# The PEER stage of a two-block kernel: top-k per token tile, last gate tile read by VectorE first, column gating and the split of h in pieces between the v columns

## The reference, cut to what matters

```python
def chunk(xc):                                      # 128 tokens
    q = (xc @ w_pq).reshape(P_CHUNK, P_HEADS, 2, P_DK // 2)
    s = jnp.einsum('thpd,hpkd->thpk', q, sub_keys)
    s_top, i_top = lax.top_k(s, P_TOPK)
    cand = s_top[..., 0, :, None] + s_top[..., 1, None, :]
    best, ci = lax.top_k(cand.reshape(P_CHUNK, P_HEADS, P_TOPK * P_TOPK), P_TOPK)
    e1 = jnp.take_along_axis(i_top[..., 0, :], ci // P_TOPK, axis=-1)
    e2 = jnp.take_along_axis(i_top[..., 1, :], ci % P_TOPK, axis=-1)
    expert = e1 * N_KEYS + e2
    gate = jax.nn.softmax(best.astype(jnp.float32), axis=-1).astype(xc.dtype)
    act = jax.nn.gelu(jnp.einsum('thkd,td->thk', u_tab[expert], xc), approximate=False)
    return jnp.einsum('thk,thkd->td', gate * act, v_tab[expert])
```

## Time and profile before

| | |
|---|---|
| median of three runs | 1895.78 us (1894.33 to 1897.16) |
| profiled execution, own time | 1899.66 us |
| profiled execution, span from first to last instruction | 1897.6 us |
| TensorE (PE) | busy 95% of the span |
| VectorE (DVE) | busy 54% |
| ScalarE (ACT) | busy 33% |
| GpSimd (POOL) | busy 8% |
| mean granted TensorE clock, as a share of full speed | 0.978 |
| scores | 464.95 to 472.3 us of the span |
| early u on TensorE | 473.47 to 598.05 us |
| gates and middle u on TensorE | 604.80 to 747.6 us |
| early v on TensorE | 751.95 to 928.8 us |
| main columns on TensorE | 928.8 to 1309.7 us |

### The profile page before, as it was taken

One profiled execution on the slowest core, in us unless ns is written; L12 is line 12 of the kernel. 1 busy time (PEld: TensorE's weight loads), 2 busy tenths in 40 slices (PEclk: granted clock), 3 DMA queues, 4 the chain that ended last, 5 costly groups with the idle time before them and its releaser, 6 DMA issues. The chain is left out here.

```text
span 1897.6 us, 23793 instructions
## 1 busy us (share of the span) xinstructions
PE 1806.9 (95%) x9024; PEld 1404.1 (74%) x9024; DVE 1031.9 (54%) x2060; ACT 623.3 (33%) x891; POOL 159.4 (8%) x81
## 2 busy tenths in 40 slices
PE   7999989999998999899999999998997979999997
PEld 4887556778887998677888888887776868555554
DVE  2669745220998876777776767675324532411112
ACT  2110354012012665333454545454264130122222
POOL 1100000000002996100000000000000000000000
PEclk9999999999999999999999999999998999899998
DMA  9366121333441223455555555556322244399992
GB/s 365 148 252 266 67 89 45 133 108 137 173 159 67 89 89 103 163 181 195 178 185 191 184 192 181 194 179 237 129 101 89 89 166 191 137 424 427 428 427 84
DMA packets 33335, 343.61 MB, mean 181 GB/s; under 512 B 3952, under 2 KB 4464, under 8 KB 5104
## 3 DMA queue, kind: packets, MB, share of 16 engines
q1 hardware_dynamic: 32256, 340.16, 47.5%
q10 hardware_dynamic: 1008, 2.45, 0.3%
HBM read 340.49 MB, written 2.10 MB: 181 GB/s over the span
## 5 line engine op out<-in xcount | busy, mean ns | idle before, releaser
L554 PE MATMUL psD<-xh,ring 128*128 128x256 f32 x1856 | 411.0, 382 | 8.9 <-DVE arena L2037 5.6
L554 PEld LDWEIGHTS psD<-xh,ring 128*128 128x128 f32 x1856 | 351.5, 191 | 67.0 <-issue 15.4
L839 PE MATMUL psY<-ring_r,work_r 128*128 128x512 f32 x1536 | 370.6, 397 | 11.2 <-DVE ring_r L1825 11.2
L839 PEld LDWEIGHTS psY<-ring_r,work_r 128*128 128x128 f32 x1536 | 283.1, 190 | 80.7 <-issue 18.0
L1122 ACT ACTIVATE arena<-psD 128x512 f32<-128x512 f32 (+4 forms) x187 | 132.2, 715 | 616.1 <-PE psD L554 473.2
L1122 ACT ACTIVATE ring_r<-ring 128x1024 fp32r<-128x1024 f32 x196 | 200.2, 1055 | 173.5 <-PE psY L839 113.1
L825 PE MATMUL psD<-xh_r,ring_r 128*128 128x512 f32 x544 | 194.1, 397 | 0.0
L554 PE MATMUL psD<-arena,ring 128*128 128x256 f32 x704 | 167.6, 398 | 12.2 <-DMA ring<-in_w_in 4.8
L1825 DVE TENSOR_TENSOR ring_r<-ring,ring_r 128x1024 fp32r<-128x1024 f32 x128 | 160.7, 1255 | 15.1 <-ACT ring_r L1122 15.0
L554 PEld LDWEIGHTS psD<-arena,ring 128*128 128x128 f32 x704 | 133.6, 192 | 44.7 <-issue 8.8
L827 PE MATMUL psD<-xh_r,ring_r 128*128 128x256 f32 x544 | 152.6, 280 | 0.0
(11 more groups left out here) (264 smaller groups left out, 1999.6 us busy)
## 6 DMA issues: line engine op xcount, KB each, us to landing
ring<-in_tables SPq DMA_DIRECT2D x68, 1024.0 KB, 4.8
arena<-in_experts SPq DMA_DIRECT2D x30, 2048.0 KB, 16.4
ring<-in_w_in SPq DMA_DIRECT2D x20, 2048.0 KB, 8.5
ring<-in_experts SPq DMA_DIRECT2D x18, 2048.0 KB, 14.3
ring<-in_early_v SPq DMA_DIRECT2D x30, 1024.0 KB, 4.8
ring<-in_w_mod SPq DMA_DIRECT2D x12, 2048.0 KB, 8.3
ring<-in_early_u SPq DMA_DIRECT2D x9, 2048.0 KB, 7.9
ring<-in_mid_u SPq DMA_DIRECT2D x12, 1024.0 KB, 4.9
```

The source lines that it names most:

```text
L554: last = nc.tensor.matmul(dst, a, b, start=(i == 0), stop=(i == len(pairs) - 1))
L839: last = nc.tensor.matmul(psY[:, t * D + h * 512:t * D + (h + 1) * 512], wgt[:, b, t * P:(t + 1) * P], v[:, h * 512:(h + 1) * 512], start= ...
```

## The change

The top-k of token tile 0 may begin when its four score tiles are copied, not all eight; the wait for all eight moves to the first place that overwrites their source. The exponentials of token tile 1 are taken two GELUs earlier. Both settings of `psY` to zero go; instead the first matmul into each bank of `psY` overwrites it (`start=first and i == 0`). TensorE does 17 instead of 6 middle steps before the first gate product and 5 or 6 before each of the others (`mid_done`, `LEAD`). After the last gate product VectorE reads `psD` first and ScalarE second, where it was the other way round, and the first v columns' rounding and rest stand before it. The gating of the middle columns goes from three instructions of 8 columns to two of 4 and eight of 2, one behind a v column. The split of `h` goes from two instructions to sixteen, each over an eighth of `h`, and each waits for a certain v column (`v_done`). The constants of the waits on these semaphores follow.

```diff
@@ tensor: gates and middle u @@
+def mid_done(n):
+    return LEAD + (MID * K - LEAD) * n // (T // 8) if n else 0      # LEAD = 12
...
-            pe.wait_ge(y_zero, 1)
             for n in range(T // 8):
-                for i in range(MID * K * n // (T // 8), MID * K * (n + 1) // (T // 8)):
+                for i in range(mid_done(n), mid_done(n + 1)):
                     mid_step(i)
@@ tensor: v columns @@
-                    for wgt, v in ((wgt_hi, v_hi[b]), (wgt_hi, v_lo), (wgt_lo, v_hi[b])):
+                    for i, (wgt, v) in enumerate(((wgt_hi, v_hi[b]), (wgt_hi, v_lo), (wgt_lo, v_hi[b]))):
...
-                                                    start=False, stop=False, skip_group_check=True)
+                                                    start=first and i == 0, stop=False, skip_group_check=True)
...
-            pe.wait_ge(y_zero, 2)
-            with pe.Fori(0, PRE // 4) as it:
+            pe.wait_ge(mid_ready, MID // 2)
+            for e in range(8):
+                early_v(e, e, e == 0)
+            with pe.Fori(1, PRE // 4) as it:
...
-            pe.wait_ge(h_split, 1)
+            pe.wait_ge(h_split, K)
@@ scalar @@
-            act.wait_ge(tile_free["act"], readers[:TILE["scores"] + 8].count("act"))
-            act.sem_inc(sc_ready, 1)
+                if g == 3:
+                    act.wait_ge(tile_free["act"], readers[:TILE["scores"] + n + 1].count("act"))
+                    act.sem_inc(sc_ready, 1)
...
-                if n in (TOPU // 3, TOPU // 2 - 1):
-                    t = n // (TOPU // 2 - 1)
+                if n in (TOPU // 3, TOPU // 2 - 3):
+                    t = n // (TOPU // 2 - 3)
...
-                gates_out(it, h)
+                if n + 1 < T // 8:
+                    gates_out(it, h)
                 if n + 2 < T // 8:
                     one_hot(it + 1, h)
+                else:
+                    act.wait_ge(col_loaded[0], 16 + MID_LOADS[0])
+                    act.wait_ge(gb_done, n + 3)
+                    fn(v_hi[h], early_half(col_slot, h), ACT.Copy).then_inc(v_hi_ready, 1)
+            gates_out(T // 16 - 1, 1, early_gated)
@@ gpsimd @@
-            pool.wait_ge(mid_gated, 2)
             pool.wait_ge(mid_used, MID // 2)
-            nc.gpsimd.tensor_copy(h_hi, hT).then_inc(h_hi_ready, 1)
-            pool.wait_ge(h_hi_ready, 1)
-            nc.gpsimd.tensor_tensor(h_lo, hT, h_hi.bitcast(F32), ALU.subtract).then_inc(h_split, 1)
+            pool.wait_ge(mid_gated, 6)
+            for k in range(K):
+                pool.wait_ge(v_done, 12 + 2 * k)
+                nc.gpsimd.tensor_copy(h_hi[:, k, :], hT[:, k, :]).then_inc(h_hi_ready, 1)
+                pool.wait_ge(v_done, 13 + 2 * k)
+                pool.wait_ge(h_hi_ready, k + 1)
+                nc.gpsimd.tensor_tensor(h_lo[:, k, :], hT[:, k, :], h_hi[:, k, :].bitcast(F32),
+                                        ALU.subtract).then_inc(h_split, 1)
@@ vector @@
-            dve.wait_ge(sc_ready, 1)
...
             for t in range(TT):
+                dve.wait_ge(sc_ready, t + 1)
...
-            dve.wait_ge(stat_used, STATS.index("x1") + 1)
-            nc.vector.memset(psY[:, :], 0.0).then_inc(y_zero, 1)
...
             gate_early(T // 16 - 1, 0)
-            dve.wait_ge(mid_ready, MID // 2)
-            nc.vector.memset(psY[:, 1024:2048], 0.0).then_inc(y_zero, 1)
-            gate_early(T // 16 - 1, 1)
-            dve.wait_ge(gate_copied, T // 8 + 2)
...
+            early_rest(0, 0)
+            gate_early(T // 16 - 1, 1, gb_done)
             dve.wait_ge(early_gated, T // 8 + 2)
-            for e in range(8):
-                early(e, e, False)
-                if e in (1, 3, 5):
-                    mid_gate((2, 0, 1)[e // 2])
-            dve.wait_ge(mid_gated, 3)
-            with dve.Fori(1, PRE // 4) as it:
+            for e in range(2):
+                weights_split(e, e, gate_all[:, e, :])
+                if e:
+                    early_rest(1, 1)
+            dve.wait_ge(gate_copied, T // 8 + 2)
+            dve.wait_ge(mid_ready, MID // 2)
+            mid_gate(2, 0, 4)
+            for e in range(2, 16):
+                early(e, e % 8)
+                if e == 2:
+                    mid_gate(2, 4, 4)
+                if 4 <= e < 12:
+                    mid_gate((e - 4) // 4, 2 * (e % 4), 2)
+            dve.wait_ge(mid_gated, 10)
+            with dve.Fori(2, PRE // 4) as it:
```

58 lines of the change are left out of this document (30 added, 28 removed).

## The result

The changed kernel takes 1880.44 us (median of 5 runs, 1874.07 to 1882.78), the kernel before 1896.07 us (5 runs in turn with them, 1894.33 to 1900.3). The ratio is 0.9904, with a 95% interval of 0.9888 to 0.9919. The forecast was 1877.9 us with a range of 1873.5 to 1885.5.

What follows compares the result with a forecast made beforehand. TensorE has work in 95% of the span, so only its pauses and low-clock stretches can be won. Gains of 20.75 less losses of 2.85 give net 17.9, from 1895.78 to 1877.9 us, range 1873.5 to 1885.5.

Steps and rivals of the forecast that it cites:

- The hand-over: From early u to the gates: first middle step starts near 600.8 instead of 604.80, 4.0 us gained.
- The first middle steps at the lower clock: First 12 passes of middle steps after the hand-over: 2.55 us back if the clock stays up in the shorter pause.
- Last gate product to column 0: Between the last gate product and v column 0: VectorE reads first, column 0's rest already done; 2.65 us less.
- The clock behind it: First v columns after the last gate product: low clock level there costs 2.3 us, won if it stays up.
- The split of h: In the v columns: TensorE's pause for GpSimd's split, 6.85 us, and the slow clock after it, 2.4, both go.
- The pieces: Sixteen pieces of the split between v columns: 0.24 hides, 0.57 just doesn't; 0.1 for each of eight, 0.8 us lost.
- The gating in pieces: Middle columns' gating among the v columns: second 1.15 us piece does not fit; 0.3 us lost, 0 to 0.6.
- Fourth load, end of the loop: Fourth v load starts a column or two later, over 9 us before use; TensorE never waited in the gate loop.
- The stall in pieces: Rival, v columns: pieces each hold TensorE up, costing 6.45 instead of 0.8; net 12.3, 1883.5 us; 12%.
- Falls in both pauses: Rival, hand-over and before column 0: clock falls in both, 2 × 2.4 instead of 1.75; net 14.9, 1880.9 us; 20%.
- A late hand-over: Rival, early u to gates: tile 1's numbers come late anyway, so 4.0 and 2.55 are missing; 1884.4 us; 5%.
- a loop bound by GpSimd: Rival, gate loop: contention pushes GpSimd to 5.0 us a step, loop 25 us longer; net −7, 1903 us; 3%.

Runs made afterwards that it cites:

- e6: Changed kernel with the old hand-over: tile 1's exponentials behind the last GELU and the memset of psY restored, earlier top-k kept; 1886.47 us, ratio 0.9941.
- e8: Changed kernel with the top-k waiting for all eight score tiles again; 1880.65 us, ratio 0.991.
- run 16: Not a label of a run: the words say that TensorE had executed 16 matmuls of 128x2 ahead of a pause; no measured time belongs to it.
- e2: Changed kernel with h split by two whole instructions again, after v column 7, instead of sixteen pieces; 1885.03 us, ratio 0.9936.
- e5: Changed kernel with LEAD = 0, so 6 instead of 17 middle steps before the first gate product; 1882.4 us, ratio 0.9913.
- e4: Changed kernel with the last gate tile read in the old order, ScalarE first, then VectorE; 1882.47 us, ratio 0.9925.
- e10: e4 with matmuls on constants added in TensorE's pause before v column 0, their result overwritten; 1883.58 us, ratio 0.9921.
- e1: Kernel before with one part of the change alone, the split of h in sixteen pieces between v columns; 1893.39 us, ratio 0.9972.
- e3: Changed kernel with the sixteen pieces released by VectorE's rest of a v column instead of TensorE's end of one; 1880.06 us, ratio 0.9899.
- e7: Changed kernel with the middle columns gated by three instructions of 8 columns again; 1878.16 us, ratio 0.9896.
- e9: Changed kernel run once more, unchanged; 1880.3 us, ratio 0.9917.
- e11: e3 plus middle steps moved into the hand-over's pauses, two before the transposes and fifteen behind, not waiting for pick; 1876.22 us, ratio 0.9892.

## Why the prediction was right, step by step

The time lies in the range, 2.5 us above the forecast of 1877.9. The net was forecast at 17.9; it is 15.6 between the medians and 19.2 between the profiled executions. The mechanisms were right but for one sign, and several sizes were off both ways, so that the sum came out closer than its terms is in part luck.

- **The hand-over, 4.0.** Right: 4.16, and e6 puts exactly this back. That it rests on the exponentials and the memset together, with the earlier top-k as cover only, was right too (e8: 0.03).
- **The first middle steps at the lower clock, 2.55.** 2.50 in this profile. But it comes back only when the clock stays up in the new pause, which it did in four of nine profiles; otherwise 1.69 of it is lost again. I had set 1.75 against one of two places in every execution. The size was right; the hand-over has it in five of nine profiles, and the place ahead of column 0 in none of nine. The pause of the earlier trace rows on which I based this was a weaker guide than I took it for: right ahead of it TensorE had run 16 matmuls of 128x2 (192.85 to 194.80), and in e2's profile the clock doesn't fall there. That is why the forecast's net is 1.3 smaller than the profile's difference: +1.75 for a fall that this profile did not have, −0.7 in early v, the rest small.
- **The lead costs nothing and is cover.** Right: without it a pause of 1.82 (e5).
- **Last gate product to column 0, 2.65.** Right: 2.67, of which ScalarE's copy is 1.42 (e4); the rest was argued from rows.
- **The clock behind it, 2.3.** Right in size and cause: columns 0 to 2 take 8.52 and not 10.53, with the pause at 3.11 the fall costs 2.4 (e4), and e10's profile, with the same late column 0 and the clock up, has 2.34 less.
- **The split of h, 6.85 + 2.4.** The mechanism was right (e2). The size of the first term was not: 0.91 of the 6.84 was the delay of the whole gating, which stays when the split goes (e1). The split's own pause is 5.3 to 5.9. By these terms, 6.84 + 2.4 − 0.91 − 1.4 = 6.9, e1 should have won more than the 6.26 it did. Of the 0.65, about 0.4 is the third gating and the rest the pieces, 1.66 there. Without the pieces the split gave back 7.9 and not 9.25: this term was 1.3 too large.
- **The pieces, 0.8.** Mis-sized: 1.4 (e3). I took an eighth of the whole instruction, 0.24 and 0.57; they take 0.40 and 0.74. The hiding place was also read wrongly. The 0.54 us that VectorE has free ends with the signal on which the pieces start, so not even the small one hides in it.
- **The gating in pieces, a loss of 0.3, not below 0.** The sign was wrong: a gain of 1.1 (e7). VectorE's total is the same, as I argued, but the whole instruction of 2.29 overran the slack of its column and was already being paid for, under the split's pause. In early v three errors, 1.3 too much for the split, 0.6 too little for the pieces and 1.4 too little for the gating, largely cancel: 10.45 less was forecast, 9.76 measured. That the sum held is luck.
- **Fourth load, end of the loop.** Right: no wait for the load, and the loop stayed TensorE's.

Early v is also the sum of the parts: 6.26 (e1) + 2.4 (the clock, e4) + 1.09 (e7) = 9.75, against 9.76. The parts are not known to the hundredth (column 0 itself went from 5.00 to 2.84, which is 2.16 and not 2.4), so the sum shows that no large part is missing, and no more.

**The rivals.** The stall in pieces fell: VectorE's column rests stay at 1.22 and the pieces cost 1.4 and not 6.45. Falls in both pauses: seen at the first, in five of nine, and never at the second. A late hand-over and a loop bound by GpSimd fell outright.

**The medians.** They differ by 15.6 and 15.1 (e9's series), less than 19.2. The profiled execution before is 3.6 above the median of its five runs, the profiled one after is at its median; that is the whole difference between 19.2 and 15.6. Executions with a fall at the hand-over give back 1.7, which this profile of after doesn't show. The rest lies in stages that the change doesn't touch: over the profiles the end of early u varies from 593.7 to 599.9 and the rest behind the early columns from 965.05 to 971.96. Ahead of early u the variation goes with the clock between 190 and 265 us. Here is that stretch in e2's profile, which ends early u first, and in after's:

```profile
190.00:265.00 75.00, 67.00 (x263) 37.49 (x262) 48.88 (x91) 34.69 (x63) 0.00 (x0) 1.00 0.26 98
190.00:265.00 75.00, 67.85 (x242) 37.98 (x242) 47.51 (x88) 34.05 (x61) 0.00 (x0) 0.93 0.26 98
```

Over all thirteen profiles, early u ends at 593.70 where this clock is 1.00, at 594.35 and 594.36 where it is 0.98, from 597.50 to 598.05 at 0.93, from 597.58 to 598.82 at 0.91, and at 598.83 and 599.94 at 0.89. What makes it fall there in one execution and not in the next was not tried, and for the part behind the early columns the traces show no such order. My correction of 3.9 us for the profiled execution before rested on three runs: against the medians of the later series, 1895.4 to 1897.9 over 11 to 13 runs, it would be 1.8 to 4.3.

## What to carry to other kernels

A pause measured on the critical path holds everything that was late at that moment, not only the last releaser: before a stall is priced, list the other instructions that overran in the same column, since they surface when the large one goes. Small work on GpSimd that shares VectorE's time was cheaper behind VectorE's instruction, on its signal, than on the signal that starts both: 1.4 us over sixteen pieces. And a pause of TensorE has a second price in those executions in which the clock falls, 1.7 to 2.5 us here: moving independent matmuls into the pause saved both in e11's profile. Whether matmuls without use save the second stays open on one profile (e10).

## What the runs showed of the hardware

- A pause of 2.59 us, broken by 0.88 us of transposes, was followed by a fall from 2.4 to 1.2 GHz in five profiles of nine of nearly or exactly the same instructions there, for 1.69 us each. After 3.11 it fell in e4's profile (2.4 us); after 1.67 to 1.69 in none of nine.
- With six matmuls on constants, 2.74 us, in a pause of 3.11, the clock stayed at 1.00 in e10's one profile; without them it fell in e4's one profile.
- GpSimd's instructions over 128x256 take 0.40 (cast) and 0.74 (subtract); over 128x2048, 1.90 and 4.56. An eighth would be 0.24 and 0.57. An estimate from the two sizes is that 0.19 us of each instruction is fixed.
- VectorE's cast of 128x256 takes 0.29 alone, and 0.83 or 0.47 when GpSimd's piece started 0.07 ahead of it. Where the cast started 0.05 ahead, it took 0.29, and GpSimd's subtract 0.85 and not 0.74.
- In 40 us of unbroken "busy" of TensorE there lie 170 matmuls in one kernel and 176 in another at the same granted clock.
- At a granted clock of 0.50 a v matmul (128x512) starts every 0.43 us (e4), at 1.00 every 0.23 (after).
